# Two-block layer stack, attention units in another order: a context unit behind every four token units, short and long units in turn

## What is computed

```python
def _softmax_attend(q, k, v):
    s = einsum('bqhd,bkhd->bhqk', q, k) * (q.shape[-1] ** -0.5)
    return einsum('bhqk,bkhe->bqhe', softmax(s), v)

# even layer, local attention: 8 heads of 64, window of +-128 tokens, the 256 context keys, and a sink
p = softmax(concat([where(|qpos - kpos| <= 128, q k_loc, NEG), q k_ctx, sink]))[..., :-1]
# the same layer for the 256 context rows: context keys and the sink alone
# even layer, differential attention: 4 heads, two score maps each
p = softmax(q k)          # tokens: 1024 + 256 keys; context rows: 256 keys
a = p[:, :, 0] - lam * p[:, :, 1];   y = a @ v
# second block, dilated attention: 8 heads of 64, causal; tile t of 128 queries sees (t + 1) * 128 keys
```

## Time and profile before

| | |
|---|---|
| median of three runs | 2624.97 us |
| span of the profiled execution | 2621.0 us |
| PE busy | 2561.3 us (98%) |
| DVE busy | 1524.4 us (58%) |
| ACT busy | 800.9 us (31%) |
| POOL busy | 223.3 us (9%) |
| chain that ended last, by engine | PE 93%, DVE 3%, ACT 2%, issue 1% |

### The profile page before, as it was taken

How to read it: one execution, slowest core, us unless ns; L and a number is a source line. 1 busy time by engine, 2 the same in 40 slices (tenths; PEclk the granted TensorE clock), 3 DMA queues, 4 the chain that set the end, 5 groups by cost and what they waited for, 6 DMA issues and landing times.

```text
span 2621.0 us, 37526 instructions
## 1 busy us (share of the span) xinstructions
PE 2561.3 (98%) x14026; PEld 1876.9 (72%) x14026; DVE 1524.4 (58%) x3904; ACT 800.9 (31%) x1756; POOL 223.3 (9%) x401
## 2 busy tenths in 40 slices
PE   6999999999999999999999999999999999999999
PEld 3477688777778685466688777868678776545867
DVE  2357677599866664344453476657768574515554
ACT  2236511176721123322210066113212264121211
POOL 0100000000011000000042021200000002012000
PEclk9999999999999999999999999999999999999999
DMA  7121000022013130211001010622240104316321
GB/s 261 27 104 49 22 33 33 33 73 76 14 49 112 65 105 32 101 41 41 9 25 39 33 48 29 98 80 90 103 145 33 69 18 111 109 62 243 102 107 56
DMA packets 73059, 188.77 MB, mean 72 GB/s; under 512 B 6989, under 2 KB 9745, under 8 KB 71953
## 3 DMA queue, kind: packets, MB, share of 16 engines
q0 software_dynamic: 26656, 94.84, 11.4%
q1 hardware_dynamic: 45472, 91.16, 9.9%
q10 hardware_dynamic: 752, 0.38, 0.0%
HBM read 143.69 MB, written 43.01 MB: 71 GB/s over the span
## 4 chain that ended last, share of the span: by engine, by line
PE 93%; DVE 3%; ACT 2%; issue 1%; DMA 0%; ACTq 0%; DVEq 0%
PE psum L1391 36%; PE psum L1723 12%; PE psum L1663 8%; PE psum L1736 7%; PE psum L1754 5%; PE psum L1751 4%; PE psum L1832 4%; PE psum L1605 3%; PE psum L1505 3%; PE psum L1377 2%; PE psum L1358 1%; PE psum L1904 1%; PE psum L1922 1%; PE psum L1891 1%; PE psum L1638 1%
## 5 line engine op out<-in xcount | busy, mean ns | idle before, releaser
L3206 ACT ACTIVATE RP<-RP,small 128x1280 f32<-128x1280 f32 (+11 forms) x274 | 252.7, 923 | 199.1 <-DVE small L2751 199.0
L1723 PE MATMUL psum<-RQ 64*128 64x256 f32 (+5 forms) x1344 | 296.0, 498 | 2.0 <-DVE small L2751 1.2
L2751 DVE CUSTOM_DVE_ANT_0 RP<-psum,small 128x512 f32<-128x512 f32 (+1 forms) x382 | 201.8, 574 | 110.1 <-PE psum L1736 86.5
L1663 PE MATMUL psum<-RW,hT 128*128 128x512 f32 (+2 forms) x640 | 237.8, 527 | 1.0 <-ACT hT L2956 1.0
L1723 PEld LDWEIGHTS psum<-RQ 64*128 64x128 f32 (+1 forms) x1344 | 145.6, 188 | 88.7 <-issue 57.4
L1736 PE MATMUL psum<-ident,RP 128*128 128x128 f32 x1388 | 192.3, 280 | 8.7 <-DVE RP L2765 3.6
L1663 PEld LDWEIGHTS psum<-RW,hT 128*128 128x128 f32 x640 | 135.2, 215 | 87.5 <-issue 69.8
L1391 PE MATMUL psum<-RW,hT 128*128 128x256 f32 x864 | 196.0, 379 | 0.0
L3219 ACT ACTIVATE RP<-psum 128x512 f32<-128x512 f32 (+1 forms) x304 | 154.0, 525 | 136.5 <-PE psum L1736 125.9
L1736 PEld LDWEIGHTS psum<-ident,RP 128*128 128x128 f32 x1388 | 151.4, 141 | 61.0 <-issue 52.5
L1391 PEld LDWEIGHTS psum<-RW,hT 128*128 128x128 f32 x864 | 163.8, 190 | 25.0 <-issue 2.4
(11 more groups left out here) (485 smaller groups left out, 3941.7 us busy)
## 6 DMA issues: line engine op xcount, KB each, us to landing
RW<-in_w_in SPq DMA_DIRECT2D x7, 2048.0 KB, 7.8
RW<-in_od_w_ada SPq DMA_DIRECT2D x6, 2048.0 KB, 8.0
RW<-in_ev_w_in SPq DMA_DIRECT2D x5, 2048.0 KB, 7.7
RW<-in_od_w_in SPq DMA_DIRECT2D x5, 2048.0 KB, 7.9
RQ<-in_ev_w_ada SPq DMA_DIRECT2D x4, 2048.0 KB, 19.4
RX<-in_x POOLq DMA_DIRECT2D x12, 512.0 KB, 7.3
y_even<-YR POOLq DMA_DIRECT2D x20, 256.0 KB, 2.3
RP<-y_even POOLq DMA_DIRECT2D x20, 256.0 KB, 3.7
```

What stands on the lines that cost most here:

```text
L1663: last = pe.matmul(main.bank(f)[:, 0:nc_], lhs_of(st["lhs"], j["t"], kk), w, start=kk == 0, stop=kk == kn - 1)
L1723: last = pe.matmul(main.bank(f)[:, 0:pc["w"]], q, kk[:, keys], start=i == 0, stop=i == len(u["qk"]) - 1)
L2751: drained(main, dve.tensor_tensor_reduce(pair_slot(st, u, lane)[:, pc["at"]:pc["at"] + pc["w"]], main.bank(f)[:, 0:pc["w"]], add, -scale, ...
L3206: fn(pr, pr, ACT.Exp, bias=mins[:, at, lane, n - 1:n], scale=-1.0, accum_out=sums[:, at, lane:lane + 1]).then_inc(s_pexp, 1)
```

## The change

The planner gets three new orders and more homes for open blocks.

- `context_between` puts one context unit behind each four token units in the local and the differential stage: units 4, 9, 14, ... 39 are the context units. The last unit is a context unit, as before.
- The dilated stage takes a unit of a short tile and one of a long tile in turn: t = 0 with 7 for the four head pairs, then 1 with 6, 2 with 5, 3 with 4.
- As two blocks are now open at once, a block gets a home from its name (`block`), not from a running number. A context block has home 2 in the local stage (in `RQ`) and in the differential stage (in `RX`); the dilated stage has four homes in turn (two more in `gate`). `s_ystore` has four semaphores; the wait before a home is used again counts the stores of that home.
- The columns of `temp` in the differential stage go by the unit's number instead of its head. `y_blocks_until`, which nothing calls, goes.

No instruction's shape or count changes: each stage has the same units. The three modulations and the five keep their numbers, and stand beside other units now.

```diff
@@ plan_pairs
                 if u["first"]:
-                    block_count[0] += 1
-                u["block"] = block_count[0] - 1
+                    home = 2 if kind in ("window", "diff") and u["t"] >= NT else opened % among
+                    opened += home == opened % among
+                    blocks[u["block"]] = home, homes_taken[home]
+                    homes_taken[home] += 1
+                u["home"], u["stored"] = blocks[u["block"]]
...
+        def context_between(pairs):
+
+            tokens_of, context_of = pairs[:4 * NT], pairs[4 * NT:]
+            return [u for i, c in enumerate(context_of) for u in tokens_of[4 * i:4 * i + 4] + [c]]
...
-        stages.append(plan_pairs("window", pairs, HD ** -0.5, [even_rows]))
+        stages.append(plan_pairs("window", context_between(pairs), HD ** -0.5, [even_rows]))
...
-        att_diff = plan_pairs("diff", pairs, HD ** -0.5, [odd_cols])
+        att_diff = plan_pairs("diff", context_between(pairs), HD ** -0.5, [odd_cols])
...
-        att_dil = plan_pairs("dilated", pairs, HD ** -0.5)
+        att_dil = plan_pairs("dilated", [u for n in range(4) for short, long in zip(pairs[4 * n:4 * n + 4], pairs[28 - 4 * n:32 - 4 * n])
+                                         for u in (short, long)], HD ** -0.5)
...
-                        if u["first"] and u["block"] >= 2:
-                            dve.wait_ge(s_ystore[u["block"] % 2], 16 * (u["block"] // 2))
+                        if u["first"] and u["stored"]:
+                            dve.wait_ge(s_ystore[u["home"]], 16 * u["stored"])
```

More of the change, by code:

```diff
@@ L194, in build @@
         s_stage = sem("stage_ready")
-        s_ystore = [sem("y_block0_stored"), sem("y_block1_stored")]
+        s_ystore = [sem(f"y_block{i}_stored") for i in range(4)]
         s_yload = [sem(f"y_stage{i}_loaded") for i in range(4)]
@@ L694, in build @@
                 pieces, tiles = banded_pieces(t, lambda t, lo, hi: mask_window[:, (lo - t + 1) * P:(hi - t + 1) * P])
-                pairs.append({"t": t, "hp": hp, "first": hp == 0, "last": hp == 3, "pieces": pieces, "key_tiles": tiles,
+                pairs.append({"t": t, "hp": hp, "block": t, "first": hp == 0, "last": hp == 3, "pieces": pieces, "key_tiles": tiles,
                               "qk": [[(qaT[64 * a:64 * a + 64, hp, t * P:(t + 1) * P], kaT[64 * a:64 * a + 64, hp // 2, :])
@@ L708, in build @@
             for h in range(4):
-                pairs.append({"t": t, "hp": h, "first": h == 0, "last": h == 3, "pieces": short_first(k0, S + L - k0),
+                pairs.append({"t": t, "hp": h, "block": t, "first": h == 0, "last": h == 3, "pieces": short_first(k0, S + L - k0),
                               "key_tiles": list(range(k0 // P, NTC)),
@@ L756, in build @@
             for hp in range(2):
-                pairs.append({"t": t, "hp": hp, "first": hp == 0, "last": hp == 1, "pieces": full_pieces(0, S + L),
+                pairs.append({"t": t, "hp": hp, "block": t, "first": hp == 0, "last": hp == 1, "pieces": full_pieces(0, S + L),
                               "key_tiles": list(range(NTC)),
@@ L827, in build @@
                     pc["add"] = mask_dilated[:, m0 + pc["at"]:m0 + pc["at"] + pc["w"]]
-                pairs.append({"t": t, "hp": hp, "first": hp == 0, "last": hp == 3, "pieces": pieces,
+                pairs.append({"t": t, "hp": hp, "block": t, "first": hp == 0, "last": hp == 3, "pieces": pieces,
                               "key_tiles": list(range(t + 1)),
@@ L965, in stored_until @@
             return n
-        def y_blocks_until(stage):
-            n = [0, 0]
-            for s in stages:
-                for u in s.get("pairs", []):
-                    if u["last"]:
-                        n[u["block"] % 2] += 16
-                if s is stage:
-                    break
-            return n
         last_window_scores = [s for s in all_stages if s["kind"] == "window"][0]["pairs"][-1]["pieces"][-1]["m"][1]
```

41 lines of the change are left out of this document (23 added, 18 removed).

## The result

The changed kernel took **2643.39 us** (median of four runs, 2639.27 to 2647.92), the kernel before 2624.95 (2623.61 to 2625.51) beside it: a ratio of **1.0076, interval 1.0064 to 1.0089**. It is slower by 0.8%. The forecast was 2647.5 with a range of 2631 to 2662.

A forecast was written before the change was run, and what follows sets the result against it. PE was taken as busy nearly always, closely coupled to DVE, with only waits able to change. Differential +14, local +1.5 and dilated +7 made +22.5 on a 2621.0 span; with 4.0 to the median, 2647.5 us, range 2631 to 2662.

The forecast's parts named there:

- The period of the differential stage: Differential stage, four token units and one context unit: five intervals between first minima sum to 27.6 us, 2.7 of it waits.
- c to b1: Differential stage, from context unit c to the first token unit behind it: 4.77 us, DVE's division waiting for ACT's exponentials.
- b2 to b3: Differential stage, second to third token unit behind a context unit: DVE's full unit decides, 5.74 us against PE's 4.9.
- b3 to b4: Differential stage, third to fourth token unit behind a context unit: DVE's 5.57 us decides against PE's some 4.2.
- The stage's sum: Differential stage: seven context units at 4.2 us plus a tail of 12.6, less 25.5, less 2.2 for modulations: +14.
- The modulations: Differential stage: numbers 14, 20 and 2 stand where PE waits, hiding about 0.8 + 1.2 + 0.4 us; 2.2 taken off.
- Rival 1: All stages: waits really are filled, exponentials ending before DVE needs them; 2618 us, faster; chance 0.08.
- Rival 2: All stages balance out: DVE catches up within a differential period, which loses 0.6 to 0.9; about 2628 us; chance 0.12.
- Rival 3: Differential stage: the clock falls there too, in each of seven periods at 3.3 us, +23, 2670 us; chance 0.08.
- The local stage: Local stage: seven new waits of 0.55 us (0.15 second exponential, 0.4 bank), +3.9, less 1.4 and 0.8 gone: +1.5.
- The dilated stage: Dilated stage: PE waits for long units' exponentials, 1.17 us per t = 7 pair, 0.7 per t = 6; +7 in all.
- The head's wait: Start of the dilated stage: no earlier unit to work on, so the first long unit's transposes come some 3.1 us late.

The follow-up runs named there:

- run 4: Changed kernel with DVE combining only 640 of a token unit's 1280 columns in the differential stage: period 26.14 us (was 27.77), stage 223.16 us.
- run 6: Changed kernel with DVE combining only 256 of a token unit's 1280 columns in the differential stage: period 25.74 us, stage 219.95 us.
- run 7: Changed kernel with differential exponentials on 768 of 1280 columns, and DVE copying a dilated short unit's chunk: differential stage 230.44 us, dilated 121.80 us.
- run 8: Changed kernel with 256 of 1280 columns combined and 768 exponentiated in the differential stage: period 25.47 us, stage 218.09 us.
- run 2: Changed kernel with the local stage alone back in its old order: local stage 146.28 us, differential 236.10 us, dilated 123.22 us.
- run 9: Changed kernel with ACT's differential exponentials one unit earlier and DVE's output scaling one unit later: differential stage 239.50 us, 4.7 more.
- run 3: Changed kernel with the dilated stage alone back in its old order: dilated stage 120.20 us.
- run 10: Changed kernel with another dilated order, one short unit between two long ones: dilated stage 120.17 us.
- run 11: Changed kernel with old local and differential orders and one short dilated unit between two long ones: 2628.51 us against 2623.69 for the kernel before, ratio 1.0021.

## Why the forecast held, step by step

- **The period of the differential stage.** Forecast 4.77, 5.76, 5.74, 5.57, 5.76, sum 27.6; measured 4.77, 5.85, 5.74, 5.56, 5.85, sum 27.77. The second and fifth were 0.09 short: they are about a whole token unit of PE, 5.86. Runs 4, 6, 7 and 8 bear out the engine named for each: c to b1 shrinks with less work for ACT or for DVE, b2 to b3 and b3 to b4 with less for DVE alone, and the other two with neither, which leaves PE.
- **The stage's sum.** Seven context units at 4.33 (forecast 4.2), a tail of 12.60 (from 732.28 to 744.88; forecast 12.6), less the 25.5 of before, make 17.4. The modulations hid 3.2 instead of 2.2 (and the three terms named for them, 0.8 + 1.2 + 0.4, make 2.4). Numbers 8, 14, 20 and 26 cost 6.6 together, with the shorter period behind the last, where the old order paid 9.3: 0, 0.6, 1.5 and 0.7 less, and the prediction had nothing for number 26. Number 2, ahead of the first period, cost 1.45 instead of 1.85. That is +14.2; run 2 gives +14.3 at an equal clock, and the profiled pair +13.0 since the clock time lost at the start halved.
- **Rival 1, the waits are filled.** False: nothing was filled, and the condition it named, exponentials 1.8 earlier, is what run 9 brought about. It made things worse. My text said that nothing would then make DVE late; true, but PE was.
- **Rival 2, the stages balance out.** False by the period.
- **Rival 3, the clock falls in the stage.** False: 1.00 from 528 on, as the one short stretch of before had it. The clock stayed at its upper level through gaps inside S of 0.4 to 0.75. The rule of the Trainium skill, page "TensorE: Matmul & The Clock Gate", section "A second HAM failure mode: psum-queue depth-cycling", by which short idle times between groups can make the clock swing, does not describe this stretch: PE went through such idle times in every period for 217 us.
- **The local stage.** The sum held (+1.2 for +1.5), its parts less so. The wait of 0.15 for the second exponential never came. The wait for the third chunk's bank was 0.68 and not 0.4, but in four periods and a part (0.46) of a fifth, not in seven: 3.2 instead of 3.9.
- **The dilated stage.** A pair of t = 0 and t = 7 waits 0.92 (0.60 before the transposes, 0.32 before the small values), forecast 1.17 in one piece (the terms named for it add to a chain of 6.04, not 6.15, so to 1.07); with t = 6 it is 0.27 and 0.30, forecast 0.7. The head's wait was 2.06 + 0.60, forecast 3.1. At the same clock time lost the stage is +7.1. I had 8.5 by the rows and took 7 for the clock: the clock did help, by 1.2 to 1.6, and the rest of the difference is the pairs.

The cause in the differential stage, then: PE has 5.86 us of work for a token unit and DVE 5.57. A context unit takes work from both, but from PE in three pieces, in three intervals, because S, T and V of a unit stand beside three different units, and from DVE in two, M and D. In each of the intervals where PE has less, another engine still has a full unit's work. In a row, the context units take their work from all engines at once, and each costs 1.81 as soon as the last token units are through. In the dilated stage it is ACT's chain for a long unit that a short neighbour doesn't cover (runs 3 and 7). In the local stage run 2 shows that the order costs the 1.2 us; which wait it is, the time line suggests and no run tests.

Little of the forecast's closeness was luck, but some was. The span grew by 21.2, for 22.5 forecast; with the clock falling as long as before it would have grown by some 23.7 (1.3 more in the differential stage and 1.2 in the dilated one, an estimate). And within the differential term two errors nearly cancel: 1.2 us too little for the seven periods, and 1.0 too little for what the modulations hide.

## What to carry to other kernels

Mixing small units among large ones filled no gap here, where another engine is nearly as full as the busiest one. Before such a change compare, interval by interval along the pipeline, the work of each engine, not the sum over the period. With the second engine at 95% of the work of the first, equal units together were the better order: the change between them is paid for once. A wait on one product of an engine (an exponential, a copy) moved to its other product when their order was changed, in runs 9 and 10; what took it away in these runs was less work (4, 6, 7, 8) or another engine to do it (7). And a busy share can't tell this: PE's rose by 13.6 us with its waits.

## What was not expected of the hardware

In the dilated stage the granted clock's falls cost the same to within hundredths. In its changed order, four runs without a fall took 123.21 to 123.23, and three with 0.79 over 8 us took 124.83 to 124.86: 1.7 us of clock time lost cost 1.6. In the old order each further 1.7 cost 1.2, probably since PE waits for others in part of that stretch. At the start of the differential stage, where PE stands for DVE, they cost less still: from the first minimum of the first unit to that of the fifth it is 20.10 with nothing lost (run 11), 20.10 and 20.30 with 1.7 (run 10, the changed kernel), and 21.6 with 3.4 (before, run 2).

How long the clock fell in a run depended on when it came to the stage, down to an experiment in another stage: with all the columns combined, the differential stage lost 3.4 near its start where it began at 506.1 or 506.2 and 1.7 with a start between 507.4 and 509.5; in run 11 it began at 504.0 and lost nothing there. In the four runs in which DVE combined less it lost nothing there, wherever it began. In runs 4 and 10 the clock fell in the local stage too, which nothing in them touches there (149.56 and 149.58, with 3.4 lost, for 147.49). I can't say more of the cause. It is a reason to compare stages and not whole runs where one part of a kernel is judged by a single profile.
